# Gelu, expert weights and diagonals in two halves of eight rows, with VectorE's small steps moved behind later dot products

## The chip, the cores and the metric

The kernel runs on one core of one Trainium2 chip. Its engines are TensorE (matrix products, into PSUM), VectorE, ScalarE (functions of one argument), GpSimd (here above all the issuer of indirect DMAs) and SyncE (issuer of plain DMAs). Each runs its own instructions in order; they wait for each other through semaphores. The metric is the device time of one execution in microseconds (us), lower is better.

## The reference

Two decoder layers over 512 tokens of width 1024, all in float32. The change lies in the second half of each layer, PEER, a layer of 16,384 experts of one neuron each, of which every token picks 16 for each of 8 heads:

```python
def block(args):
    xb, ib, gb = args
    a = jax.nn.gelu(jnp.einsum('td,tkd->tk', xb, expert_u[ib]), approximate=False)
    return jnp.einsum('tk,tkd->td', a * gb, expert_v[ib])
...
for i in range(DEPTH):
    mix = hybrid_mixer(x, w_in[i], conv_w[i], b_if[i], ret_norm_g[i], mlstm_norm_g[i], w_out[i])
    x1 = layer_norm(DN_ALPHA * x + mix, ln1_g[i], ln1_b[i])
    y = peer(x1, peer_wq[i], peer_keys[i], peer_u[i], peer_v[i])
    e = jax.nn.sigmoid(x1 @ ple_wg[i] + ple_bg[i]) * (p[i] @ ple_wp[i])
    x = layer_norm(DN_ALPHA * x1 + y + e, ln2_g[i], ln2_b[i])
```

`ib` holds the expert numbers a token picked, `gb` the softmax weights of its picks. Each pick costs one row of `expert_u` and one of `expert_v`, 4 KB each: 512 x 128 x 2 rows a layer, 537 MB.

## The kernel before

**Tiles and loops.** Tokens lie on the 128 partitions, so there are 4 blocks of 128. A *pair* n = 0 to 31 is one block (n // 8) and one head (n % 8); it has 16 *rows* k, the 16 picks of every token. For one row GpSimd gathers a 128 x 1024 tile of U (`gather_u`, L558) and later one of V (`gather_v`, L567), 512 KB each, into two rings of 8 tiles (`UR`, `VR`). A U slot is free again when VectorE has done its dot product (semaphore `u_free`), a V slot when TensorE (`v_free`) or VectorE (`v_added`) has used it.

**One pair through the engines.** VectorE multiplies each U tile with the block's x and sums along the row (`dot_products`, L1066; x stands in PSUM as `xps`, put there by ScalarE's `copy_x`, L613 and L614, once a block). After 16 dots ScalarE takes Gelu of all 16 (L607), VectorE multiplies with the softmax weights (`weights`, L1088 and L1091), and ScalarE makes from each of the 16 columns a diagonal 128 x 128 matrix (L795). TensorE multiplies the diagonal with the V tile and adds up in PSUM (L1610, two products of 512 columns a row, four records in the trace), over all 8 heads of a block. GpSimd's order is fixed: in loop n it issues u(n+1,k), v(n,k) for k = 0 to 15. So V rows of pair n arrive while VectorE does the dots of pair n+1.

**What lies between.** In loops 2 to 9 TensorE first computes the query and score products for one head of the other three blocks (L1416, L1437), which ScalarE copies out (L627, L642) after the diagonals. VectorE's top-16 search for pairs n+2 to n+4 is cut in small steps, some behind each dot (`halves_step`, `pairs_step`). In pairs 2 to 7 every fourth V row (3, 7, 11, 15; `on_vector`) is not taken by TensorE: VectorE adds it, times its weight, to `yv` (`add_row`, L1108), behind the dot of the same k of the next pair. In pair 31 it takes every second row. `PLE_AT` names eight pairs in which the embedding term e is computed for half a block's columns: TensorE (L1571 to L1575) before the pair's V rows, ScalarE's sigmoid (L805), VectorE's multiply and add (`add_ple`, L1339, L1343 or L1345) after the pair's dots. `LN_AT` names three pairs with a final LayerNorm; ScalarE's square root for it stands at the end of the loop. `add_y` (L1325, L1327) takes the finished sum of a block out of PSUM. In pair 1 ScalarE's loop begins with the queries and scores of heads 4 to 7 and the transposes of three blocks, before Gelu.

The two ends that the prediction follows are these: `gelu` waits for `u_free` at 16 (n + 1), and `weights(n)` stands at the end of `dot_products(n)` and waits for `gelu_done`:

```python
e.wait_ge(gelu_done, n + 1)
e.scalar_tensor_tensor(wgt[:, n % 2, :], act_d, grec[:, 0:1], gexp[:, b, :], ALU.mult, ALU.mult).then_inc(wgt_ready, 1)
```

## Time and profile before

| What | us |
|---|---|
| timed runs: median of 3 (lowest, highest) | 3441.97 (3438.99, 3443.26) |
| profiled execution: span, first to last instruction | 3781.1 |
| TensorE matmul busy | 3004.2 |
| VectorE busy | 2120.8 |
| GpSimd busy | 1984.4 |
| ScalarE busy | 676.8 |

The page gives no time around the span. Its mean granted TensorE clock is 0.933 of full. The DMA engines moved 1174.41 MB, 311 GB/s over the span; the 2,048 gathers carry 1073.87 MB of it. In the page's slices one sees two stretches with little DMA traffic (the mixers, about 300 us each at the start of a layer) and two long ones near full (PEER, about 1,500 us each). The chain that ended last is spread over all engines (TensorE 27%, VectorE 18%, GpSimd 16%, issue 15%, DMA 9%), as it is where a ring of buffers couples them.

### The profile page before, as it was taken

How to read it: one execution, taken by the hardware profiler on the slowest of the kernel's cores; microseconds unless marked ns; L12 is line 12 of the kernel's file. 1: busy time of each engine (PE TensorE's matmuls, PEld its weight loads, DVE VectorE, ACT ScalarE, POOL GpSimd, SP SyncE). 2: the span in 40 equal slices, each digit the busy share in tenths (PEclk: the TensorE clock that was granted, in tenths of full speed). 3: DMA queues.
4: the chain of work that ended last, by engine and by line, in shares of the span. 5: the costliest groups of instructions: out<-in, count | busy, mean ns of one | idle time of the engine just before them, and what ended most of it. 6: DMA issues, size and time to landing. Idle time of an engine off the chain costs nothing.

```text
span 3781.1 us, 25835 instructions
## 1 busy us (share of the span) xinstructions
PE 3004.2 (79%) x7696; PEld 1341.3 (35%) x7696; DVE 2120.8 (56%) x4948; ACT 676.8 (18%) x1658; POOL 1984.4 (52%) x2100
## 2 busy tenths in 40 slices
PE   8999777778778888777699987777777788887776
PEld 4555433333223323222245544333322233333222
DVE  1447665575555655665424476665656555656654
ACT  1331111111111112111013211111111111121110
POOL 0014455566665666666500145555566666666665
PEclk9999888889999999999999998888899999999999
DMA  4127899998999999999831278998899999989998
GB/s 153 67 70 256 313 342 344 346 350 338 399 368 351 355 384 355 348 371 367 336 129 67 70 269 316 353 347 339 335 363 407 363 352 363 385 329 362 371 370 321
DMA packets 360799, 1174.41 MB, mean 311 GB/s; under 512 B 36946, under 2 KB 75986, under 8 KB 360404
## 3 DMA queue, kind: packets, MB, share of 16 engines
q0 software_dynamic: 294912, 1073.87, 74.7%
q1 hardware_dynamic: 63284, 98.59, 7.6%
q8 instruction: 61, 1.00, 0.1%
q10 hardware_dynamic: 2464, 0.31, 0.1%
q14 instruction: 78, 0.64, 0.0%
HBM read 1170.54 MB, written 2.10 MB: 310 GB/s over the span
## 4 chain that ended last, share of the span: by engine, by line
PE 27%; DVE 18%; POOL 16%; issue 15%; another core or an unknown queue 11%; DMA 9%; ACT 4%; DVEq 1%; ACTq 0%; SPq 0%; POOLq 0%
DVE arena L1066 10%; POOL arena L567 9%; PE bank L1610 8%; POOL arena L558 8%; DMA arena<-in_peer_v,rows 5%; PE bank L1389 5%; DMA arena<-in_peer_u,rows 4%; PE yv L1389 3%; ACT arena L795 3%; PE bank L1416 2%; PE yv L1547 1%; PE bank L1437 1%; PE yv L1467 1%; PE bank L1547 1%
## 5 line engine op out<-in xcount | busy, mean ns | idle before, releaser
L1610 PE MATMUL bank<-arena 128*128 128x512 f32 x3840 | 1906.7, 637 | 523.0 <-DMA arena<-in_peer_v,rows 318.4
L1066 DVE CUSTOM_DVE_ANT_0 arena<-arena,xps 128x1024 f32<-128x1024 f32 x1024 | 1237.4, 1214 | 629.3 <-DMA arena<-in_peer_u,rows 464.2
L567 POOL DMA_INDIRECT arena<-in_peer_v,rows x1024 | 974.6, 952 | 714.1 <-issue 281.8
L1610 PEld LDWEIGHTS bank<-arena 128*128 128x128 f32 x3840 | 719.3, 200 | 1696.4 <-issue 938.4
L558 POOL DMA_INDIRECT arena<-in_peer_u,rows x1024 | 972.5, 950 | 552.1 <-issue 293.0
L607 ACT ACTIVATE arena<-arena 128x16 f32<-128x16 f32 x64 | 13.9, 218 | 1897.9 <-issue 1160.9
L795 ACT ACTIVATE arena<-keep,arena 128x128 f32<-128x128 f32 x960 | 294.2, 388 | 299.1 <-remote 147.8
L1416 PE MATMUL bank<-xT,arena 128*128 128x128 f32 (+1 forms) x1024 | 250.2, 399 | 57.4 <-issue 55.5
L1416 PEld LDWEIGHTS bank<-xT,arena 128*128 128x128 f32 x1024 | 165.3, 203 | 132.5 <-issue 72.3
L1389 PE MATMUL bank<-arena,xT 128*128 128x512 f32 (+1 forms) x448 | 187.1, 573 | 6.4 <-DMA arena<-in_w_in 4.3
L1389 PE MATMUL yv<-arena,xT 128*128 128x512 f32 (+1 forms) x320 | 132.6, 569 | 0.0
L1437 PE MATMUL bank<-arena 128*128 128x128 f32 x192 | 46.9, 434 | 100.5 <-ACTq L628 90.8
L1339 DVE TENSOR_TENSOR arena<-arena,bank 128x512 f32<-128x512 f32 x16 | 11.0, 687 | 195.3 <-ACTq L806 118.1
L1389 PEld LDWEIGHTS bank<-arena,xT 128*128 128x128 f32 x448 | 84.9, 193 | 99.8 <-issue 90.7
L1571 PE MATMUL bank<-arena,xT 128*128 128x512 f32 x256 | 112.5, 592 | 0.0
L544 POOL TENSOR_TENSOR arena<-arena,normg 128x256 f32<-128x256 f32 x8 | 5.8, 726 | 189.7 <-ACTq L719 189.7
L1437 PEld LDWEIGHTS bank<-arena 128*128 128x128 f32 x192 | 42.2, 329 | 119.2 <-ACTq L628 106.0
L1066 DVE DVE_READ_ACCUMULATOR2_ANT arena<- 128x1 f32 x1024 | 84.1, 82 | 0.0
L1389 PEld LDWEIGHTS yv<-arena,xT 128*128 128x128 f32 x320 | 60.9, 195 | 62.1 <-issue 60.5
L540 POOL MEMSET arena<- 128x3 f32 x8 | 0.4, 101 | 142.5 <-PE xps L1485 142.5
L1571 PEld LDWEIGHTS bank<-arena,xT 128*128 128x128 f32 x256 | 48.6, 190 | 61.2 <-issue 61.2
L1547 PE MATMUL yv<-arena,xT 128*128 128x512 f32 x160 | 69.7, 592 | 0.0
(288 smaller groups left out, 1966.1 us busy)
## 6 DMA issues: line engine op xcount, KB each, us to landing
arena<-in_peer_wq SPq DMA_DIRECT2D x32, 1024.0 KB
arena<-in_w_in SPq DMA_DIRECT2D x12, 2048.0 KB, 8.0
arena<-in_peer_u,rows POOLq DMA_INDIRECT x1024
arena<-in_peer_v,rows POOLq DMA_INDIRECT x1024
arena<-in_w_out SPq DMA_DIRECT2D x4, 2048.0 KB, 8.2
arena<-in_ple_wg SPq DMA_DIRECT2D x4, 2048.0 KB
arena<-in_mixer SPq DMA_DIRECT2D x2, 2112.0 KB, 19.4
ln<-in_ln SPq DMA_DIRECT2D x8, 512.0 KB, 7.9
```

Source lines behind the costliest of these rows:

```text
L558: e.indirect_dma_start(urow[i % UR], None, a["peer_u"], bass.IndirectOffsetOnAxis(ap=rows[:, n % RR, k:k + 1], axis=0)).then_inc(u_in[i % ...
L567: e.indirect_dma_start(vrow[i % VR], None, a["peer_v"], bass.IndirectOffsetOnAxis(ap=rows[:, n % RR, k:k + 1], axis=0)).then_inc(v_in[i % ...
L607: e.activation(act_d, dots[:, n % 2, :], ACT.Gelu).then_inc(gelu_done, 1)
L795: e.activation(diag[:, k, :], ident, ACT.Copy, scale=wgt[:, n % 2, k:k + 1]).then_inc(diag_ready, 1)
L1066: e.tensor_tensor_reduce(r, r, xps[:, :], 1.0, 0.0, ALU.mult, ALU.add, dots[:, n % 2, k:k + 1]).then_inc(u_free, 1)
L1389: ins = e.matmul(ps[:, 0:w], xT[:, k, i * P:(i + 1) * P], wt[:, k, :], start=(k == 0), stop=(k == KT - 1))
L1416: ins = e.matmul(ps[:, at:at + hi - lo], wq[m % 2][:, k, n * P:(n + 1) * P], xT[:, k, lo:hi], start=(k == 0), stop=(k == KT - 1))
L1437: ins = e.matmul(ps[:, b * NKEYS:(b + 1) * NKEYS], qT[:, s, b * P:(b + 1) * P], keys[m % KR][:, s, :], start=True, stop=True)
L1467: ins = e.matmul(ps[:, :], wt[:, k, i * P:(i + 1) * P], xT[:, k, :], start=(k == 0), stop=(k == KT - 1))
L1547: ins = e.matmul(ps[:, :], xT[:, k, b * P:(b + 1) * P], wt[:, k % 4, side * 512:(side + 1) * 512], start=(k == 0), stop=(k == KT - 1))
L1571: e.matmul(ps[:, :], xT[:, k, b * P:(b + 1) * P], wg[:, k, :], start=(k == 0), stop=False)
L1610: ins = e.matmul(bank[m][:, :], diag[:, k, :], vrow[i % VR][:, m * 512:(m + 1) * 512], start=(h == 0 and k == 0), stop=(h == PH - 1 and k ...
```

## The change

- Gelu, `weights` and the diagonals are done for rows 0 to 7 and 8 to 15 apart (`HALF`), the first half already within the pair. In `dot_products(n)` VectorE does `weights(n, 0)` behind dot 9 and `weights(n-1, 1)` behind dot 1 (`WEIGHT_ROW`); only pairs 0 and 31 differ.
- The embedding's `add_ple` stands behind dot 5 of the next pair (`PLE_ROW`).
- In pairs 2 to 7 VectorE takes V rows 0, 4, 8, 12, and adds row k behind dot k + 3 (`VLAG`).
- ScalarE's order in loop n: Gelu and diagonals of the first half, Gelu of the second, `copy_x` of the next block (before: at the head of the next loop), the LayerNorm's square root (before: at the loop's end), diagonals of the second half.

```diff
@@ -67,2 +67,4 @@
 SR, RR, PC = 5, 6, D // 2
+HALF = TOPK // 2
+WEIGHT_ROW, VLAG, PLE_ROW = 1, 3, 5
 
@@ -462,6 +464,6 @@
         def on_vector(i):
-            return i % VD == VD - 1 if VFIRST <= i < VLAST else i >= VHALF and i % 2 == 1
+            return i % VD == 0 if VFIRST <= i < VLAST else i >= VHALF and i % 2 == 1
 
         def vector_rows(i):
-            return max(0, min(i, VLAST) - VFIRST) // VD + max(0, i - VHALF) // 2
+            return (max(0, min(i, VLAST) - VFIRST) + VD - 1) // VD + max(0, i - VHALF) // 2
 
@@ -603,6 +605,19 @@
 
-                def gelu(n):
+                def gelu(n, s):
 
-                    e.wait_ge(u_free, (n + 1) * TOPK)
-                    e.activation(act_d, dots[:, n % 2, :], ACT.Gelu).then_inc(gelu_done, 1)
+                    lo, hi = s * HALF, (s + 1) * HALF
+                    e.wait_ge(u_free, n * TOPK + hi)
+                    e.activation(act_d[:, lo:hi], dots[:, n % 2, lo:hi], ACT.Gelu).then_inc(gelu_done, 1)
+
+                def diagonals(n, s):
+
+                    e.wait_ge(wgt_ready, 2 * n + s + 1)
+                    for k in range(s * HALF, (s + 1) * HALF):
+                        if on_vector(n * TOPK + k):
+                            continue
+                        if n > 0 and on_vector((n - 1) * TOPK + k):
+                            e.wait_ge(v_free, tensor_rows((n - 1) * TOPK + k))
+                        elif n > 0:
+                            e.wait_ge(v_free, tensor_rows((n - 1) * TOPK + k) + 1)
+                        e.activation(diag[:, k, :], ident, ACT.Copy, scale=wgt[:, n % 2, k:k + 1]).then_inc(diag_ready, 1)
 
@@ -754,3 +769,4 @@
                             choice(1)
-                            gelu(0)
+                            gelu(0, 0)
+                            gelu(0, 1)
                         elif i == (3, 0):
@@ -763,4 +779,2 @@
                 for n in range(PAIRS):
-                    if n % PH == 0 and n > 0:
-                        copy_x(n // PH)
                     steps = pair_steps(n)
@@ -785,12 +799,12 @@
                     if n > 0:
-                        gelu(n)
-                    e.wait_ge(wgt_ready, n + 1)
-                    for k in range(TOPK):
-                        if on_vector(n * TOPK + k):
-                            continue
-                        if n > 0 and on_vector((n - 1) * TOPK + k):
-                            e.wait_ge(v_free, tensor_rows((n - 1) * TOPK + k))
-                        elif n > 0:
-                            e.wait_ge(v_free, tensor_rows((n - 1) * TOPK + k) + 1)
-                        e.activation(diag[:, k, :], ident, ACT.Copy, scale=wgt[:, n % 2, k:k + 1]).then_inc(diag_ready, 1)
+                        gelu(n, 0)
+                    diagonals(n, 0)
+                    if n > 0:
+                        gelu(n, 1)
+                    if n % PH == PH - 1 and n + 1 < PAIRS:
+                        copy_x(n // PH + 1)
+                    if n in LN_AT:
+                        e.wait_ge(var_ready, 3 + NB + LN_AT[n])
+                        e.sqrt(rstd[:, 0:1], rstd[:, 0:1]).then_inc(std_ready, 1)
+                    diagonals(n, 1)
                     for step, i in steps:
@@ -810,5 +824,2 @@
                         choice(n + 3)
-                    if n in LN_AT:
-                        e.wait_ge(var_ready, 3 + NB + LN_AT[n])
-                        e.sqrt(rstd[:, 0:1], rstd[:, 0:1]).then_inc(std_ready, 1)
                 e.wait_ge(var_ready, 2 + 2 * NB)
@@ -1079,14 +1090,21 @@
                             pairs_step([n + 2, n + 3], k, i + 1)
-                        if n > 0 and on_vector((n - 1) * TOPK + k):
-                            add_row(n - 1, k, i + 1)
-                    e.drain()
-
-                def weights(n):
-
-                    b = n % NB
-                    e.wait_ge(gexp_ready, n + 1)
-                    e.reciprocal(grec, gsum[:, b:b + 1])
-                    e.drain()
-                    e.wait_ge(gelu_done, n + 1)
-                    e.scalar_tensor_tensor(wgt[:, n % 2, :], act_d, grec[:, 0:1], gexp[:, b, :], ALU.mult, ALU.mult).then_inc(wgt_ready, 1)
+                        if n > 1 and k == WEIGHT_ROW:
+                            weights(n - 1, 1)
+                        if n > 0 and k == HALF + WEIGHT_ROW:
+                            weights(n, 0)
+                        if n > 0 and k >= VLAG and on_vector((n - 1) * TOPK + k - VLAG):
+                            add_row(n - 1, k - VLAG, i + 1)
+                        if k == PLE_ROW and n - 1 in PLE_AT:
+                            add_ple(PLE_AT[n - 1])
+                    e.drain()
+
+                def weights(n, s):
+
+                    b, lo, hi = n % NB, s * HALF, (s + 1) * HALF
+                    if s == 0:
+                        e.wait_ge(gexp_ready, n + 1)
+                        e.reciprocal(grec, gsum[:, b:b + 1])
+                        e.drain()
+                    e.wait_ge(gelu_done, 2 * n + s + 1)
+                    e.scalar_tensor_tensor(wgt[:, n % 2, lo:hi], act_d[:, lo:hi], grec[:, 0:1], gexp[:, b, lo:hi], ALU.mult, ALU.mult).then_inc(wgt_ready, 1)
                     e.drain()
@@ -1102,3 +1120,3 @@
                         e.drain()
-                    elif i == VFIRST + VD - 1:
+                    elif i == VFIRST:
                         e.tensor_scalar(yv[:, :], vrow[i % VR], w, None, ALU.mult).then_inc(v_added, 1)
@@ -1351,3 +1369,4 @@
                         first_norm(1)
-                        weights(n)
+                        weights(n, 0)
+                        weights(n, 1)
                         halves_first([2, 3])
@@ -1356,8 +1375,6 @@
                         pairs_second([2, 3])
-                    else:
-                        weights(n)
+                    elif n == PAIRS - 1:
+                        weights(n, 1)
                     if n % PH == 0 and n > 0:
                         add_y(n // PH - 1)
-                    if n in PLE_AT:
-                        add_ple(PLE_AT[n])
                     if n in LN_AT:
@@ -1603,2 +1620,4 @@
                         i = n * TOPK + k
+                        if k % HALF == 0:
+                            e.wait_ge(diag_ready, tensor_rows(i + HALF))
                         if on_vector(i):
@@ -1606,6 +1625,4 @@
                         e.wait_ge(v_in[i % VR], (l * (PAIRS * TOPK // VR) + i // VR + 1) * 16)
-                        if k % (2 * VD) == 0:
-                            e.wait_ge(diag_ready, tensor_rows(i + 2 * VD))
                         for m in range(2):
-                            ins = e.matmul(bank[m][:, :], diag[:, k, :], vrow[i % VR][:, m * 512:(m + 1) * 512], start=(h == 0 and k == 0), stop=(h == PH - 1 and k == (TOPK - 2 if b in (0, NB - 1) else TOPK - 1)))
+                            ins = e.matmul(bank[m][:, :], diag[:, k, :], vrow[i % VR][:, m * 512:(m + 1) * 512], start=(h == 0 and k == 0), stop=(h == PH - 1 and k == (TOPK - 2 if b == NB - 1 else TOPK - 1)))
                         ins.then_inc(v_free, 1)
```

Three places show what the edits do to the order. The first is VectorE in pair 1, from its tenth dot (the row with u_in1) in the change, and from its fourteenth (u_in5) before; a dot is the row `arena<-arena,xps` and the `128x1` behind it; `RECIPROCAL` and the product behind it are the weights. Before:

```order
L1066 ISA arena<-arena,xps 128x1024 [waits u_in5]
L1066 ISA arena 128x1
L991 TENSOR_TENSOR arena<-arena 128x512 [waits u_free]
L1066 ISA arena<-arena,xps 128x1024 [waits u_in6]
L1066 ISA arena 128x1
L996 CAST arena<-topi 128x64 [waits u_free]
L1066 ISA arena<-arena,xps 128x1024 [waits u_in7]
L1066 ISA arena 128x1
L1088 RECIPROCAL arena<-arena 128x1 [waits gexp_ready]
L1091 SCALAR_TENSOR_TENSOR arena<-arena 128x16 [waits gelu_done]
L1066 ISA arena<-arena,xps 128x1024 [waits u_in0]
```

In the change (other line numbers, same functions):

```order
L1077 ISA arena<-arena,xps 128x1024 [waits u_in1]
L1077 ISA arena 128x1
L969 MAX_INDEX topi<-arena 128x8 [waits u_free]
L970 MAX_INDEX topi<-arena 128x8
L973 MAX_INDEX topi<-arena 128x8 [waits u_free]
L974 MAX_INDEX topi<-arena 128x8
L1106 RECIPROCAL arena<-arena 128x1 [waits gexp_ready]
L1109 SCALAR_TENSOR_TENSOR arena<-arena 128x8 [waits gelu_done]
L1077 ISA arena<-arena,xps 128x1024 [waits u_in2]
L1077 ISA arena 128x1
L977 MATCH_REPLACE arena<-arena 128x128 [waits u_free]
```

The wait for `gelu_done` stood behind the sixteenth dot (u_in7) and stands behind the tenth; six dots of pair 1 now come after it.

The second is VectorE at the end of pair 17, with the embedding's multiply and add (the product that waits for `ple_gate`). Before, it comes behind the last dot (u_in7) and the weights:

```order
L1066 ISA arena<-arena,xps 128x1024 [waits u_in7]
L1066 ISA arena 128x1
L1088 RECIPROCAL arena<-arena 128x1 [waits gexp_ready]
L1091 SCALAR_TENSOR_TENSOR arena<-arena 128x16 [waits gelu_done]
L1339 TENSOR_TENSOR arena<-arena,bank 128x512 [waits work_full1,ple_gate]
L1343 TENSOR_TENSOR acc<-acc,arena 128x512
L1066 ISA arena<-arena,xps 128x1024 [waits u_in0]
```

In the change it is in pair 18, behind that pair's sixth dot (u_in5):

```order
L1030 MAX arena<-arena 128x8 [waits u_free]
L1031 MAX arena<-arena 128x8
L1077 ISA arena<-arena,xps 128x1024 [waits u_in5]
L1077 ISA arena 128x1
L1034 MAX_INDEX pos<-arena 128x8 [waits u_free]
L1357 TENSOR_TENSOR arena<-arena,bank 128x512 [waits work_full1,ple_gate]
L1361 TENSOR_TENSOR acc<-acc,arena 128x512
L1077 ISA arena<-arena,xps 128x1024 [waits u_in6]
```

Six dots and their small steps moved ahead of it. The third is ScalarE in loop 7 and at the head of loop 8: Gelu, diagonals, the copies of query and score, and the two copies of x. Before:

```order
L607 ACTIVATE arena<-arena 128x16 [waits u_free]
L795 ACTIVATE arena<-keep,arena 128x128 [waits v_free,wgt_ready]
L795 ACTIVATE arena<-keep,arena 128x128 [waits v_free] x11
L627 COPY arena<-bank 128x384 [waits work_full0,work_full1]
L627 COPY arena<-bank 128x384 [waits work_full1]
L642 COPY arena<-bank 128x3x128 [waits work_full0]
L642 COPY arena<-bank 128x3x128 [waits work_full1]
L613 COPY xps<-x 128x512 [waits u_free]
L614 COPY xps<-x 128x512
L607 ACTIVATE arena<-arena 128x16 [waits u_free]
L795 ACTIVATE arena<-keep,arena 128x128 [waits v_free,wgt_ready]
```

In the change:

```order
L610 ACTIVATE arena<-arena 128x8 [waits u_free]
L622 ACTIVATE arena<-keep,arena 128x128 [waits v_free,wgt_ready]
L622 ACTIVATE arena<-keep,arena 128x128 [waits v_free] x5
L610 ACTIVATE arena<-arena 128x8 [waits u_free]
L628 COPY xps<-x 128x512 [waits u_free]
L629 COPY xps<-x 128x512
L622 ACTIVATE arena<-keep,arena 128x128 [waits v_free,wgt_ready]
L622 ACTIVATE arena<-keep,arena 128x128 [waits v_free] x5
L642 COPY arena<-bank 128x384 [waits work_full0,work_full1]
L642 COPY arena<-bank 128x384 [waits work_full1]
L657 COPY arena<-bank 128x3x128 [waits work_full0]
L657 COPY arena<-bank 128x3x128 [waits work_full1]
```

The copies of x (`xps<-x`) moved from behind the diagonals and four copies of query and score to just behind the second Gelu.

## Rows read from the trace of the kernel before

**Rows 1.** The page: busy us (share, instructions) and GB/s in 40 slices.
```profile
PE 3004.2 (79%) x7696; PEld 1341.3 (35%) x7696; DVE 2120.8 (56%) x4948; ACT 676.8 (18%) x1658; POOL 1984.4 (52%) x2100
GB/s 153 67 70 256 313 342 344 346 350 338 399 368 351 355 384 355 348 371 367 336 129 67 70 269 316 353 347 339 335 363 407 363 352 363 385 329 362 371 370 321
```
**Rows 2.** Windows (busy us by engine, clock, DMA share, GB/s): a calm stretch, and one around a pause.
```profile
1044.00:1076.00 32.00, 23.83 (x49) 8.13 (x48) 22.01 (x47) 4.82 (x16) 24.07 (x27) 1.00 1.01 396
1079.00:1095.00 16.00, 10.55 (x23) 3.67 (x22) 9.21 (x30) 3.66 (x7) 8.75 (x10) 1.00 0.84 293
```
**Rows 3.** Timeline (start us, us, engine, line; idle before, releaser), GpSimd, u(17,15).
```profile
1196.64 0.94 POOL L558 DMA_INDIRECT arena<-in_peer_u,rows  x1 [0.31 <-issue]
```
**Rows 4.** Timeline, VectorE and GpSimd, behind a pause.
```profile
1081.47 0.09 DVE L966 MATCH_VALUE_LOAD arena<-arena 128x8 f32 x1 [2.97 <-issue]
1081.71 0.94 POOL L567 DMA_INDIRECT arena<-in_peer_v,rows  x1 [3.77 <-issue]
```
**Rows 5.** Timeline, VectorE, end of pair 17: last dot, embedding's multiply.
```profile
1203.11 1.22 DVE L1066 CUSTOM_DVE_ANT_0 arena<-arena,xps 128x1024 f32<-128x1024 f32 x1 [1.33 <-DMA arena<-in_peer_u,rows]
1225.03 0.69 DVE L1339 TENSOR_TENSOR arena<-arena,bank 128x512 f32<-128x512 f32 x1 [20.12 <-ACTq L806]
```
**Rows 6.** Timeline, GpSimd, u(18,8).
```profile
1228.13 0.94 POOL L558 DMA_INDIRECT arena<-in_peer_u,rows  x1 [4.31 <-DVE arena L1066]
```
**Rows 7.** Waits (us, times, longest), GpSimd, pairs 16 to 25, layers one and two.
```profile
POOL arena L558 <- DVE arena L1066: 30.6, 14, 6.3
POOL arena L558 <- DVE arena L1066: 34.0, 21, 7.3
```
**Rows 8.** Timeline, TensorE, pair 17: embedding and its bias product.
```profile
1206.23 7.03 PE L1571 MATMUL bank<-arena,xT 128*128 128x512 f32 x16
1213.19 1.12 PE L1572 MATMUL bank<-arena,keep 1*128 1x512 f32 x2
```
**Rows 9.** Timeline, ScalarE, pair 17: Gelu and sigmoid.
```profile
1204.37 0.22 ACT L607 ACTIVATE arena<-arena 128x16 f32<-128x16 f32 x1 [27.18 <-issue]
1224.37 0.60 ACT L805 ACTIVATE arena<-bank 128x512 f32<-128x512 f32 x1
```
**Rows 10.** Timeline, VectorE, pair 1: dots 10 and 15, weights.
```profile
406.50 1.20 DVE L1066 CUSTOM_DVE_ANT_0 arena<-arena,xps 128x1024 f32<-128x1024 f32 x1
418.96 1.21 DVE L1066 CUSTOM_DVE_ANT_0 arena<-arena,xps 128x1024 f32<-128x1024 f32 x1
436.68 0.24 DVE L1091 SCALAR_TENSOR_TENSOR arena<-arena 128x16 f32<-128x16 f32 x1 [12.71 <-ACT arena L607]
```
**Rows 11.** Timeline, ScalarE, pair 1: a query's copy, and Gelu.
```profile
413.95 0.37 ACT L623 COPY arena<-bank 128x256 f32<-128x256 f32 x1 [12.23 <-remote]
436.42 0.22 ACT L607 ACTIVATE arena<-arena 128x16 f32<-128x16 f32 x1
```
**Rows 12.** Timeline, GpSimd, u(2,2) and u(2,9).
```profile
409.22 0.93 POOL L558 DMA_INDIRECT arena<-in_peer_u,rows  x1 [0.30 <-issue]
444.80 0.94 POOL L558 DMA_INDIRECT arena<-in_peer_u,rows  x1 [0.30 <-issue]
```
**Rows 13.** Waits of the whole span.
```profile
PE bank L1610 <- ACT arena L795: 59.2, 21, 7.9
DVE arena L1091 <- ACT arena L607: 26.1, 2, 13.4
```
**Rows 14.** Timeline, VectorE and GpSimd, first dot of pair 8 and u(8,8).
```profile
751.41 1.22 DVE L1066 CUSTOM_DVE_ANT_0 arena<-arena,xps 128x1024 f32<-128x1024 f32 x1 [23.32 <-ACT xps L614]
752.91 0.93 POOL L558 DMA_INDIRECT arena<-in_peer_u,rows  x1 [12.05 <-DVE arena L1066]
```
**Rows 15.** Timeline, TensorE and GpSimd: first V row of pair 6, v(6,8); first V row of pair 7.
```profile
699.29 4.05 PE L1610 MATMUL bank<-arena 128*128 128x512 f32 x8
701.90 0.94 POOL L567 DMA_INDIRECT arena<-in_peer_v,rows  x1 [8.68 <-PE bank L1610]
...
749.44 6.72 PE L1610 MATMUL bank<-arena 128*128 128x512 f32 x13
```

## The prediction

> **What bounds the kernel now.** I read the busy rows of the page first: the expert stage of each layer (from about 320 to 1876 us, and again from 2200) keeps the 16 DMA engines near full, up to 407 GB/s [rows 1]. A window of a calm stretch shows what full means: 396 GB/s at a DMA share of 1.01 [rows 2]. Then GpSimd's timeline: it issues 2,048 gathers of 512 KB, and in calm stretches one every 1.24 us, 0.94 busy and 0.30 between [rows 3]. A pair of gathers (one U row, one V row) therefore cannot start faster than every 2.49 us, and at 396 GB/s its 1.05 MB take 2.65. The two limits stand so close that a GpSimd stall is not made up: what GpSimd waits beyond 0.30 us is lost, except where another chain is later anyway. The question for each edit is which GpSimd wait it ends or starts.
>
> One thing must be set aside. At 1081.5 us GpSimd, VectorE and ScalarE all come back from a pause, GpSimd having idled 3.77 us, VectorE 2.97 [rows 4], while VectorE waited only for its own dot product; in the 16 us around it DMA moves 293 GB/s [rows 2]. The profiled span is 3781.1 us (the page gives nothing around it), the median of the timed runs 3441.97: 339 us less. Such pauses recur through the whole stage, and 339 us is 90 of them at 3.77; so I take most of them to belong to the profiled execution. Gaps in the trace then bound a gain from above, and I rebuild the two chains that matter without pauses.
>
> **The change, part by part.** Notation: dot(n,k) is row k of pair n, u(n,k) and v(n,k) its gathers. GpSimd issues u(n+1,k), then v(n,k); each has a ring of eight.
>
> *Embedding later (8 pairs a layer).* At the end of pair 17 the last dot starts at 1203.11 and ends 1.2 later; the embedding's multiply starts at 1225.03 after 20.12 us of idle time [rows 5], and the next dot 1.6 us behind it. GpSimd had room to u(18,7) and then waited 4.31 us for that dot [rows 6]. By the view of waits over the ten pairs 16 to 25 these waits are 30.6 us (14) in layer one and 34.0 (21) in layer two [rows 7]; less 35 x 0.30, 54 us in all. That is the upper bound of this part: after the change VectorE has the multiply behind dot(n+1,5), 15 us later, and nothing stalls. Without pauses: TensorE starts the embedding at 1206.23, its bias product ends at 1213.19 + 1.12 = 1214.3 [rows 8], the sigmoid takes 0.60 (it stands at 1224.37 here, 10 us after its input) [rows 9], the two VectorE steps 1.6: the next dot would start at 1216.5 and end at 1217.7. GpSimd's u(18,8) would be due nine steps after u(17,15), at 1196.6 [rows 3]: 1196.6 + 9 x 2.49 = 1219.0. So in an execution free of pauses this stall is nothing, with 1.3 us to spare. Bounds 0 and -54. The timed runs have most of the 339 us less, not surely all, and eight to ten near misses a layer turn into stalls with any delay; I take -22, between the ends and nearer zero.
>
> *VectorE's wait for Gelu moved up: the price.* Weights of the first half now stand behind dot(n,9), so dots 10 to 15 of the same pair queue behind a Gelu. In steady pairs ScalarE has been idle before it, 27.18 us in pair 17 [rows 9], and answers at once. Pair 1 is different: there ScalarE reaches its Gelu only behind four queries, four score copies and three transposes, at 436.42 [rows 11]. VectorE now runs dots 10 to 15 at 406.50 to 418.96 and waits 12.71 us after all of them [rows 10]. After the change it waits behind dot(1,9), from about 406.4, and dot(1,10) starts where dot(2,0) stands now, about 437. The u ring is what this stops: u(2,2) was issued at 409.22 and needs dot(1,10), so it comes at about 438.3. Now GpSimd stops only at u(2,8) and v(1,8), and u(2,9) comes at 444.80 [rows 12]; after, it comes at 438.3 + 7 x 2.49 = 455.7: 11 us late. TensorE's V rows of pair 1 then wait for their rows. Both layers have this wait (26.1 us in two) [rows 13]: +22. Without pauses ScalarE's Gelu would come sooner: its copy at 413.95 alone idled 12.23 us [rows 11]. If it comes at 424, the stall of u(2,2) is 425.8 - 409.2 = 16.6 us and the old one about nothing until u(2,8), due 6 x 2.49 = 15 us after u(2,2); if at 418, 10.6 us and none: 11 to 15, nearly the same. Lower bound +5 a layer (the queries' weight loads fill part of the hole), upper +15: +10 to +30 for both, taken +21.
>
> *copy_x before the diagonals.* At the end of pair 7 the next dot waits 23.32 us and GpSimd 12.05 [rows 14]. But v(7,8) behind it waits for TensorE as in every pair from 2 to 9: v(6,8) came at 701.90, 2.6 us after TensorE's first V row at 699.29, and in pair 7 that row stands at 749.44 [rows 15]. So v(7,8) would come at 752.0; now it comes one issue after 752.91, at 754.15. I take 3.5 a layer, bounds 0 and 10: -7. At 15 to 16 and 23 to 24 GpSimd never stalled: 0.
>
> *VectorE's V rows.* In pairs 2 to 7 VectorE takes rows 0, 4, 8, 12 instead of 3, 7, 11, 15, after the same dots 3, 7, 11, 15, so 24 adds a layer stay where they are. v(n,8) no longer waits for TensorE but v(n,9) does, and TensorE's last row is 15 instead of 14, with the next query right behind it: one pair-step of 2.49 won, the same lost. 0; bounds -2.5 and +2.5 for each of 12 pairs, -30 to +30, near zero because both ends belong to one loop. The lag also holds a V slot until dot k+3; the ring leaves five rows, GpSimd runs three ahead (8 us over 2.49): no wait.
>
> *Instructions.* 62 more Gelus of 0.22 us and as many small products of 0.24 [rows 9, 10]: ScalarE is 18% busy [rows 1]; the gaps between dots hide them. The number of table loads does not change; if one came with each half, 62 x 1.28 would sit on ScalarE beside 27 us of idle time, still 0. TensorE's waits for a diagonal (59.2 us in 21) [rows 13] go where the pair starts, but the V ring covers nearly all of them: -4, bounds 0 and -10.
>
> Sum on the profile: -22 + 21 - 7 + 0 - 4 = -12 us. Carried over one to one: 3442 - 12 = **3430 us**.
>
> The Trainium skill ("DMA: Bandwidth & Descriptors", section Bandwidth) puts the HBM side of a core's HBM to SBUF stream at about 358 GB/s. The trace does not agree: 396 and 407 GB/s stand in its rows. By that rule the stage would have no room at all, and the answer would be the third rival below.
>
> **Rivals.** (1) *The wait in pair 1 decides; the change is slower.* VectorE sits behind dot(1,9) in both layers and the embedding stalls were the profiler's own. For it: the rebuilt chain with its 1.3 us to spare, and a wait that no ring covers. +21 - 7 = +14: 3456 us. It decides as soon as the embedding part brings under 14 us. (2) *The stalls of the trace are real in the timed runs.* Then -54 - 7 - 4 + 21 = -44: 3398. For it: 65 us of GpSimd waits by name; against it: 339 us that the timed runs do not have. (3) *DMA is the floor.* With backlog enough the queues hide both stalls and gains: within 7 us of 3442. Windows at 396 GB/s speak for it, the page's 350 in most slices against it.
>
> **Chances.** Forecast 0.35 (3420 to 3440), rival 1 0.27, rival 2 0.20, rival 3 0.18. A difference under 0.2%, 7 us, is what measuring this kernel cannot tell from none. Faster: 0.20 + most of 0.35 = 0.50; within: 0.26; slower: 0.24. All low bounds together give about 3370, all high ones 3472 with the V rows at zero; the range with 8 in 10 is 3388 to 3462.
>
> **What would show it.** Right: in the profile after, VectorE's second-half weights and the embedding multiply have no idle time to speak of before them, and GpSimd's waits for VectorE in pairs 16 to 25 are under 15 us a layer; in pair 1 the first half's weights show 25 to 30 us of idle time, and GpSimd waits at u(2,2), about 25 us in the profile. TensorE's first V row of pairs 3 to 8 is still about 24 us behind its last one. Wrong: if GpSimd does not stop in pair 1, or if the embedding's stalls turn up at v(n,8) as waits for TensorE, which has some 9 us of embedding before each such pair's rows. A time over 3449 means rival 1; under 3405, rival 2.

## The result, and the profile after

| | us |
|---|---|
| before, 20 runs | 3439.67 (3434.43 to 3443.30) |
| after, 20 runs | 3445.84 (3440.58 to 3448.96) |
| ratio | 1.0018, 95% interval 1.0011 to 1.0024 |

The change makes the kernel 6 us slower. That is under the 0.2% named ahead, but the interval excludes no change. 3430 was forecast. The time lies in the range, on the other side of before.

The profiled execution of the changed kernel spans 3445.8 us and has no pauses. A second one of the kernel before, taken for the comparison, has none either: 3437.2 us, not 3781.1. Below, "before" is this undisturbed profile. Its page, busy times and slices, and then those of after [rows 1]:

```profile
PE 2918.5 (85%) x7696; PEld 1282.2 (37%) x7696; DVE 2136.1 (62%) x4948; ACT 669.9 (19%) x1658; POOL 1983.2 (58%) x2100
GB/s 142 75 49 182 358 406 405 404 407 394 407 409 397 407 407 400 409 409 409 358 129 73 39 218 361 405 405 405 407 399 407 409 394 408 403 404 405 409 409 343
```
```profile
PE 2920.6 (85%) x7696; PEld 1287.8 (37%) x7696; DVE 2160.6 (63%) x5012; ACT 688.7 (20%) x1722; POOL 1983.9 (58%) x2100
GB/s 142 75 49 186 345 407 404 405 398 408 407 409 406 406 407 400 407 409 409 336 135 73 32 212 353 406 405 405 396 409 407 410 402 408 404 403 405 409 409 333
```

From the sixth slice on, to the last but one of the stage, both stand at 394 to 410 GB/s: the 350 of rows 1 was the paused execution's average. What differs is the ramp (358 to 345 in the fifth slice, 361 to 353 in the second layer's) and the slice in which the stage ends (358 to 336, 343 to 333). Windows of the ramp, before and after (length, busy time of five engines, clock, DMA share, GB/s), and of the ten pairs of the embedding:

```profile
375.00:450.00 75.00, 60.03 (x252) 34.40 (x250) 55.90 (x130) 13.11 (x34) 46.44 (x49) 0.95 0.94 355
1105.00:1444.00 339.00, 305.62 (x666) 120.93 (x666) 225.14 (x528) 72.42 (x180) 242.48 (x258) 0.99 1.02 406
```
```profile
375.00:450.00 75.00, 60.11 (x248) 33.92 (x248) 53.10 (x128) 15.48 (x42) 38.29 (x41) 0.95 0.92 341
1107.00:1446.00 339.00, 305.74 (x667) 121.53 (x667) 233.92 (x536) 74.78 (x189) 245.03 (x257) 0.99 1.02 405
```

The loss is in pair 1 [rows 10 to 12]. Timelines of ScalarE, VectorE and GpSimd in the changed kernel:

```profile
413.68 0.21 ACT L610 ACTIVATE arena<-arena 128x8 f32<-128x8 f32 x1
```
```profile
413.92 0.23 DVE L1109 SCALAR_TENSOR_TENSOR arena<-arena 128x8 f32<-128x8 f32 x1 [10.99 <-ACT arena L610]
```
```profile
415.78 0.93 POOL L560 DMA_INDIRECT arena<-in_peer_u,rows  x1 [10.58 <-DVE arena L1077]
```

ScalarE comes to the half Gelu at 413.68, VectorE has stood 10.99 us for it, and GpSimd 10.58 at u(2,2). In the kernel before VectorE has done all sixteen dots by then. ScalarE waits 0.85 us for the last of them, and VectorE's weights come without idle time before them:

```profile
414.00 0.22 ACT L607 ACTIVATE arena<-arena 128x16 f32<-128x16 f32 x1 [0.85 <-DVE arena L1066]
```
```profile
414.30 0.24 DVE L1091 SCALAR_TENSOR_TENSOR arena<-arena 128x16 f32<-128x16 f32 x1
```

The embedding's part did what it says, and the waits changed their name [rows 7]. GpSimd's waits (us in total, times, longest) in pairs 16 to 25 of layer one, before and then after:

```profile
POOL arena L558 <- DVE arena L1066: 34.7, 28, 9.6
POOL arena L567 <- PE bank L1610: 7.9, 26, 0.3
```
```profile
POOL arena L569 <- PE bank L1627: 34.4, 36, 8.1
POOL arena L560 <- DVE arena L1077: 6.0, 15, 1.7
```

42.6 us before, 40.4 after. (The 7.9 us in 26 are nothing but the 0.30 us that stand before every issue.) At pair 16 a stop of 8.36 us at u(17,8) turned into one of 7.93 at v(16,8), the issue behind it, within a microsecond:

```profile
1079.23 0.94 POOL L558 DMA_INDIRECT arena<-in_peer_u,rows  x1 [8.36 <-DVE arena L1066]
```
```profile
1079.74 0.94 POOL L569 DMA_INDIRECT arena<-in_peer_v,rows  x1 [7.93 <-PE bank L1627]
```

When the last V gather of a pair lands shows what all this is worth (read from the records of the two traces, us):

```
layer one   pair 2   pair 31  between    layer two  pair 2   pair 31  between
before       499.4    1712.2   1212.8               2209.8   3422.5   1212.7
after        502.3    1715.1   1212.8               2218.4   3431.2   1212.8
```

From pair 2 to pair 31 both take the same time to 0.1 us. What is lost is lost before pair 2: 2.9 us in layer one and, counted from the landing of its first pair, 2.1 in layer two. The remaining 3.6 us of these two profiles' 8.6 lie between the layers, where the change edits nothing; they go with the granted clock, as shown behind the terms of the prediction.

### The profile page after: what moved, and what is told of

Read it like the earlier page. It is cut to its first block, busy times and chain, and to the rows that moved or that the text cites. A ratio compares the mean times of both kernels' runs of the same rounds, so it can differ in the third digit from the quotient of the medians.

```text
span 3445.8 us, 26089 instructions
## 1 busy us (share of the span) xinstructions
PE 2920.6 (85%) x7696; PEld 1287.8 (37%) x7696; DVE 2160.6 (63%) x5012; ACT 688.7 (20%) x1722; POOL 1983.9 (58%) x2100
## 4 chain that ended last, share of the span: by engine, by line
PE 39%; DMA 32%; POOL 17%; issue 7%; DVE 4%; ACT 1%; DVEq 0%; ACTq 0%; SPq 0%; POOLq 0%
DMA arena<-in_peer_v,rows 22%; PE bank L1627 12%; POOL arena L569 9%; DMA arena<-in_peer_u,rows 8%; POOL arena L560 8%; PE bank L1433 5%; PE bank L1406 5%; PE yv L1406 4%; PE bank L1588 3%; PE yv L1564 2%; DVE arena L1077 2%; PE yv L1484 1%; PE bank L1564 1%; PE bank L1592 1%; DMA arena<-in_w_in 1%
## 5 line engine op out<-in xcount | busy, mean ns | idle before, releaser
L1627 PE MATMUL bank<-arena 128*128 128x512 f32 x3840 | 1867.2, 624 | 454.1 <-DMA arena<-in_peer_v,rows 436.9
L1627 PEld LDWEIGHTS bank<-arena 128*128 128x128 f32 x3840 | 696.2, 194 | 1608.5 <-DMA arena<-in_peer_v,rows 811.4
L610 ACT ACTIVATE arena<-arena 128x8 f32<-128x8 f32 x128 | 27.0, 211 | 1301.5 <-DVE arena L1077 1301.5
L1433 PE MATMUL bank<-xT,arena 128*128 128x128 f32 (+1 forms) x1024 | 227.8, 381 | 1.9 <-ACTq L762 1.5
L1433 PEld LDWEIGHTS bank<-xT,arena 128*128 128x128 f32 x1024 | 156.0, 191 | 75.7 <-issue 9.6
L537 POOL TENSOR_TENSOR arena<-arena 128x512 f32<-128x512 f32 x8 | 10.1, 1263 | 95.4 <-DVEq L1163 95.4
L1126 DVE SCALAR_TENSOR_TENSOR yv<-arena,yv 128x1024 f32<-128x1024 f32 x46 | 58.9, 1280 | 1.3
```

Of the source, the lines that this page charges most:

```text
L610: e.activation(act_d[:, lo:hi], dots[:, n % 2, lo:hi], ACT.Gelu).then_inc(gelu_done, 1)
L1126: e.scalar_tensor_tensor(yv[:, :], vrow[i % VR], w, yv[:, :], ALU.mult, ALU.add).then_inc(v_added, 1)
L1433: ins = e.matmul(ps[:, at:at + hi - lo], wq[m % 2][:, k, n * P:(n + 1) * P], xT[:, k, lo:hi], start=(k == 0), stop=(k == KT - 1))
L1627: ins = e.matmul(bank[m][:, :], diag[:, k, :], vrow[i % VR][:, m * 512:(m + 1) * 512], start=(h == 0 and k == 0), stop=(h == PH - 1 and k ...
```

## Experiments

Each ratio is to runs of the kernel before on the same chip.

**1. The kernel before again.** 

> The kernel before, once more, for a profile to set beside that of the changed kernel, and as the measure of what 'no change' looks like. Both theories: 3440 us, ratio to before 1.000 within 0.1%. The trace of before that the prediction rested on had a span of 3781 us with 339 us of pauses in it; the theory is that these were that one execution's own, so a second profile of the same program spans 3438 us or so, its DMA slices are flat at 400 to 410 GB/s like those of the changed kernel, and GpSimd's waits for VectorE behind the embedding (30.6 and 34.0 us a layer in rows 7) shrink to under 10 us a layer. Rival: they were real, the waits stay at 30 us a layer, and then moving the embedding must have gained some 20 us that something else ate.

3440.23 us, ratio 1.0004 (0.9995 to 1.0014); span 3437.2, and the slices above. The pauses were that one execution's own. But the waits stayed (34.7 and, in layer two, 34.6 us), so neither side had it: they are real, and yet, as experiment 4 shows, their end brings no time.

**2. The wait of pair 1 taken away.**

```diff
-                        if n > 0 and k == HALF + WEIGHT_ROW:
+                        if n > 1 and k == HALF + WEIGHT_ROW:
...
+                    elif n == 1:
+                        weights(n, 0)
```

> The changed kernel with one thing undone: in the second pair the weights of the first eight rows come behind all sixteen dot products again, instead of behind the tenth. Theory A (that wait is the cause of the loss): GpSimd's stop at the u gather of the third pair's row 2 (10.6 us at 416 us and 10.0 us at 2132 us) goes, and 16 to 21 us come off: 3425 to 3430 us, which is below before too. Theory B (the DMA queues take it back: they are the floor from pair 3 on and the stop lies beside work that has to wait anyway): the stop goes but less than 5 us of the time, 3441 to 3446 us. Theory C (V rows are the cause): no change, 3446 us.

3440.07 us, ratio 1.0004 (0.9995 to 1.0013): before's time again. The stop at u(2,2) is gone. It took 5.8 us with it: theory A had the cause right and the size three times too large, and theory B, under 5 us because the DMA queues take the rest back, was the nearer one. All other parts of the change together are worth nothing that can be measured.

**3. The V rows as before** (rows 3, 7, 11, 15; `VLAG` 0; the stop flag at row 14 in the first block). 

> The changed kernel with VectorE's V rows as before: rows 3, 7, 11, 15 of pairs 2 to 7, each added right behind the dot product of its own number, instead of rows 0, 4, 8, 12 three dots later. Theory A (the wait in the second pair is the whole loss, the V rows cost nothing): GpSimd's 30 us of waits for the adds of V rows go, and the time stays within 3 us of 3446. Theory C (the slots that are held three dots longer delay the gathers behind them): 10 to 20 us come off, 3426 to 3436 us. Rival of both: row 0 on VectorE lets TensorE start later and end at row 15, so undoing it takes a gain away, 3450 us or more.

3447.01 us, ratio 1.0023 (1.0012 to 1.0034): beside after's 3445.84 nothing that eight runs between 3441.60 and 3452.68 could tell. Theory A had this right. GpSimd's waits from 460 to 770 us, after and then here:

```profile
POOL arena L569 <- PE bank L1627: 19.0, 17, 4.5
POOL arena L569 <- DVE yv L1126: 16.6, 11, 3.2
```
```profile
POOL arena L569 <- PE bank L1627: 35.8, 21, 5.9
```

35.6 us and 35.8: again the same sum under another name.

**4. The embedding's move alone,** on the kernel before:

```diff
+                        if k == 5 and n - 1 in PLE_AT:
+                            add_ple(PLE_AT[n - 1])
...
-                    if n in PLE_AT:
-                        add_ple(PLE_AT[n])
```

> The kernel before with one part of the change alone: the embedding's adds behind the sixth dot product of the next pair. In the undisturbed profile of before, GpSimd waits 60.2 us for VectorE in pairs 16 to 25 of both layers, 2.9 us in the changed kernel. Theory A (from the third pair on the DMA queues are the bound at 405 to 409 GB/s, so GpSimd's stops there cost nothing): those waits go to under 10 us, its waits for TensorE grow by about as much, and the time stays at 3438 to 3442 us. The prediction's own view (22 us for this move): 3418 us.

The reverse, only this part undone in the changed kernel, has no time: there the sigmoid that the adds need stands behind diagonals whose weights VectorE makes only after the adds, in the next pair, so the two wait for each other for ever.

3441.26 us, ratio 1.0002 (0.9993 to 1.0011). The term of 22 us is zero within 4 us. GpSimd's waits in pairs 16 to 25 of layer one, 34.5 us in all, now mostly for TensorE:

```profile
POOL arena L567 <- PE bank L1610: 27.9, 32, 8.1
POOL arena L558 <- DVE arena L1066: 6.6, 8, 4.5
```

**5. The wait of pair 1 three dots later** (`k == HALF + 4` where n is 1). 

> The changed kernel with the wait of the second pair three dot products later: its first-half weights stand behind the thirteenth dot product instead of the tenth, all else as changed. Each of these dots has two steps of the choice beside it, some 2.3 us, so VectorE reaches the wait about 9 us later and stands 2 us instead of 11.0. Theory A (a stop of GpSimd costs only what the DMA queues' backlog doesn't cover, and in the changed kernel 10.6 us of stop cost 3 us a layer): the stop at the third pair's row 2 shrinks under 3 us and the time goes to before's, 3438 to 3442 us. Theory D (not the stop but the halving itself, the extra waits and instructions, costs the 6 us): 3444 to 3447 us.

3442.15 us, ratio 1.0006 (0.9997 to 1.0015). VectorE waits 4.6 us, not 2, and GpSimd stops 3.4 us, at u(2,5) (2.5 in layer two):

```profile
413.50 0.23 DVE L1109 SCALAR_TENSOR_TENSOR arena<-arena 128x8 f32<-128x8 f32 x1 [4.61 <-ACT arena L610]
```
```profile
415.36 1.27 POOL L560 DMA_INDIRECT arena<-in_peer_u,rows  x1 [3.38 <-DVE arena L1077]
```

Most of the 6 us is gone though the halves are all there: theory D falls.

**6 and 7. ScalarE's square root ahead of head 4's copies,** on the changed kernel and on the one before. It isn't part of the change; it closes a hole that both have.

```diff
                         for b in range(2, NB):
-                            if b == NB - 1:
-                                copy_q((4, 0))
-                                copy_s((4, 0))
                             e.wait_ge(var_ready, 3 + b)
                             e.sqrt(rstd[:, 0:1], rstd[:, 0:1]).then_inc(std_ready, 1)
+                        copy_q((4, 0))
+                        copy_s((4, 0))
```

> The changed kernel with one edit of its own that is not part of the change: in the second pair ScalarE takes the square root of the last block's norm ahead of its two copies of the query and scores of head 4, not behind them. In the profiles VectorE stands 8.7 us for that root in both kernels, GpSimd 13.5 us at the second pair's u row 13, and the DMA engines are idle from 387 to 394 us. Theory A (DMA is the bound, so time comes only from where DMA stands idle): the gap closes, but here Gelu of the second pair still comes when it did (behind ScalarE's other copies, at 413.7 us), so the stop at the third pair's row 2 grows from 10.6 toward 19 us and gives most of it back: 3436 to 3444 us. Rival (the two stops don't touch each other): 8 us a layer, 3430 us.

3460.82 us, ratio 1.0062 (1.0049 to 1.0076): slower than either side had it. GpSimd's stop at u(1,13) shrinks from 13.81 us to 4.75, but VectorE then stands 7.19 us for scores and comes to its wait for Gelu only 2.4 us earlier (400.5 instead of 402.9). Gelu comes 5.9 us later, at 419.60. The third query's product sets that: its weights, asked for within 1 us of the same time, land 11.0 us after their issue instead of 6.4, and it ends at 407.65 instead of 401.73. Timelines of VectorE, GpSimd and TensorE:

```profile
419.85 0.23 DVE L1108 SCALAR_TENSOR_TENSOR arena<-arena 128x8 f32<-128x8 f32 x1 [19.36 <-ACT arena L610]
```
```profile
421.71 0.94 POOL L560 DMA_INDIRECT arena<-in_peer_u,rows  x1 [20.00 <-DVE arena L1076]
```
```profile
401.65 6.00 PE L1432 MATMUL bank<-xT,arena 128*128 128x128 f32 x32 [4.93 <-DMA arena<-in_peer_wq]
```

> The kernel before with the same edit: the square root ahead of the copies of head 4 in the second pair. Theory A (DMA the bound from the second pair to the last; a gap in it closed early is kept to the end): 7 to 8 us a layer, 3424 to 3427 us, with the landings of the V rows of every later pair 7 to 8 us earlier in the first layer. Rival (the time is set by TensorE's and VectorE's own work in pairs 2 to 9, with DMA only busy because it is asked early): less than 3 us in all, 3437 to 3440 us.

3435.69 us, ratio 0.9989 (0.9980 to 0.9998): a gain, and about a quarter of what theory A had. The hole at 387 us narrows (267 to 328 GB/s in the window from 375 to 400), but the next 50 us fall from 400 to 375. Here too VectorE now waits for Gelu in pair 1, behind its sixteenth dot, and GpSimd stops 7.29 us at u(2,8), which needs the dot behind that wait:

```profile
420.96 0.24 DVE L1090 SCALAR_TENSOR_TENSOR arena<-arena 128x16 f32<-128x16 f32 x1 [10.31 <-ACT arena L607]
```

**8 and 9. DMA taken off the bound.** In both kernels the V gathers of pairs 8 to 30 fetch 2 KB a row, and TensorE multiplies that half twice: the kernels leave out the other half of these rows, and their output is not the reference's.

```diff
+                    w = 512 if 8 <= n < PAIRS - 1 else 1024
-                    e.indirect_dma_start(vrow[i % VR], None, a["peer_v"], ...
+                    e.indirect_dma_start(vrow[i % VR][:, 0:w], None, (a["peer_v"] if w == 1024 else a["peer_v"].rearrange("r (h c) -> (r h) c", h=2)), ...
```

> The kernel before with the V gathers of pairs 8 to 30 halved (each fetches 2 KB a row instead of 4, from the first half of the table, and TensorE multiplies the same half twice, so the values of these pairs are not the reference's). It takes the DMA bound away: a pair's 16.8 MB at 408 GB/s, 41 us, become 12.6 MB, 31 us. What is left is GpSimd's own issue, 32 gathers by 0.94 + 0.30 us = 39.7 us a pair. Theory A: with DMA out of the way a stop of GpSimd costs its full length, so the kernel before keeps its 30 us a layer of waits for VectorE in pairs 16 to 25: about 2 x (23 x 1.8 - 25) = 33 us come off, 3395 to 3415 us.

> The changed kernel with the same halved V gathers in pairs 8 to 30. Theory A: here the waits for VectorE are 3 us a layer and those for TensorE no longer follow from DMA's pace, so the changed kernel is now 15 to 50 us faster than the kernel before with halved gathers: the embedding's move was worth about what the prediction gave it (22 us) or more, but only where DMA isn't the bound. Rival (the waits moved from VectorE to TensorE for a reason of their own, TensorE being late by the embedding's matmuls): both halved kernels within 8 us of each other.

3359.34 us (ratio 0.9763, 0.9748 to 0.9778) and 3364.52 (0.9773, 0.9757 to 0.9789), four runs each. The rival had the difference right (5 us, within its 8), and theory A was wrong in an instructive way: I had expected the 30 us of waits to stay in the halved kernel before and to cost their length. They are not there. Waits of GpSimd in pairs 16 to 25, halved kernel before:

```profile
POOL arena L568 <- PE bank L1611: 8.2, 27, 0.3
POOL arena L558 <- DVE arena L1067: 4.6, 15, 0.3
```

None is longer than the 0.3 us that every issue has. A pair takes 40.5 us (1084.4 to 1449.0 for nine), a little over the 32 issues of 1.24. GpSimd waits for VectorE or TensorE there only because DMA is slower than its issue: the rings must fill, and it stops at whichever row frees its slot last. The median time from issue to landing shows the queue, before and then the halved one:

```profile
arena<-in_peer_u,rows POOLq DMA_INDIRECT x1024, 10.5
arena<-in_peer_v,rows POOLq DMA_INDIRECT x1024, 10.7
```
```profile
arena<-in_peer_u,rows POOLq DMA_INDIRECT x1024, 5.6
arena<-in_peer_v,rows POOLq DMA_INDIRECT x1024, 5.0
```

**10 to 12. A version that beats both.** First the two repairs of 2 and 6 together:

> The changed kernel with the two repairs together: the second pair's first-half weights behind all its dot products, and ScalarE's square root ahead of the copies of head 4. Theory A: no wait for Gelu is left in the second pair in either form (the kernel before with the early root still had stops of 5.3 and 7.3 us at the third pair's u rows 1 and 8, partly for it), so it is below before and at or below the 3435.7 us of the kernel before with the early root: 3430 to 3436 us. If the stop at row 8 is VectorE's own work (two steps of the choice behind each dot product), it is the same as that kernel within 2 us.

3435.50 us, ratio 0.9992 (0.9983 to 1.0001): the same as experiment 7. In it VectorE still stands 8.41 us for Gelu. Then, on the changed kernel with the early root, ScalarE's order in pair 1 mended, so that Gelu comes ahead of the later copies, with VectorE's weights two dots later (ScalarE's old calls for pair 1 go; not shown):

```diff
                             copy_s(i)
+                            if n == 1 and i == (5, 0):
+                                gelu(1, 0)
+                            elif n == 1 and i == (6, 0):
+                                diagonals(1, 0)
+                            elif n == 1 and i == (7, 0):
+                                gelu(1, 1)
...
-                        if n > 1 and k == WEIGHT_ROW:
+                        if n > 1 and k == (3 if n == 2 else WEIGHT_ROW):
...
-                        if n > 0 and k == HALF + WEIGHT_ROW:
+                        if n > 0 and k == (HALF + 3 if n == 1 else HALF + WEIGHT_ROW):
```

> The changed kernel with the early square root, and with ScalarE's own order in the second pair mended instead of VectorE's wait taken away: Gelu of the first half behind the copies of heads 4 and 5, its diagonals behind those of head 6, Gelu of the second half behind those of head 7, all ahead of the copies of x; VectorE's first-half weights behind the twelfth dot product and the second-half ones behind the fourth of the next pair. In the run with both repairs VectorE still stood 8.4 us at 413 us for Gelu (ScalarE came to it at 421.6 us), and the DMA engines ran at 320 to 370 GB/s from 393 to 448 us. Theory A (time comes only from where the DMA queues run short): that stop goes, the engines stay at 400 GB/s from 393 us on, and 1 to 3 us a layer come off beside 3435.5 us: 3429 to 3434 us. If it is 3435 us or more, what limits the ramp is VectorE's own work in the second pair and the order of waits in it no longer matters.

3434.25 us, ratio 0.9984 (0.9975 to 0.9993): just outside theory A's 3429 to 3434, and beside 3435.50 no difference clear of the scatter. Last, the norm of block 3 two dots later (`LN1_AT = {1: 2, 6: 3}`):

> The same kernel, with the norm of the last block two dot products later (behind the seventh of the second pair instead of the fifth). Theory A: GpSimd's stop of 4.7 us at the second pair's u row 13 shrinks, the DMA gap at 387 us (down to 4 GB/s in one us) closes, and up to 3 us a layer more come off: 3424 to 3432 us. Rival: the gap only moves behind the norm, and the time is that of the kernel above within 2 us.

3431.56 us, ratio 0.9978 (0.9969 to 0.9988): 8.6 us under before, 14 under after, as theory A had it at the slow end. It is 2.7 us under the kernel above, hardly more than the rival's 2. GpSimd's 4.7 us at u(1,13) did not go, though: 4.56 us stand two rows later, at u(1,15), so the gap in part moved. The ramp's window in this kernel:

```profile
375.00:450.00 75.00, 62.06 (x257) 36.30 (x255) 57.40 (x134) 14.96 (x41) 48.32 (x51) 0.98 1.00 379
```

379 GB/s where before has 355 and after 341. Landings of pairs 2 and 31 in layer one: 494.5 and 1707.8, 1213.3 us between, as in the other two: the gain, too, lies ahead of pair 2.

## Why the prediction was wrong

The mechanisms were mostly named; the sum went wrong by one choice. It took every GpSimd wait as lost time ("what GpSimd waits beyond 0.30 us is lost") and left the DMA floor to rival 3. By the runs the terms are 0 for all parts but the wait in pair 1, and 5.8 for that, where 6.2 us were measured.

- **The bound** failed. The two limits do stand close, 2.49 us against 2.65, but the slower one is DMA, and it alone counts: 1212.8 us from pair 2 to 31 in both kernels, whatever GpSimd waits, and some 80 us less in all when a quarter of the bytes of 23 pairs a layer is left out (experiments 8 and 9). The 350 of rows 1, which spoke against rival 3, came from pauses that the prediction had itself set aside.
- **Embedding, -22:** zero, alone (experiment 4) and within the change (experiment 2). The rebuilt chain, "nothing, with 1.3 us to spare", holds in the halved kernel, where no stop exceeds 0.3 us. It fails in the real one, as I read it, for a reason it left out: at DMA's pace (41.8 us a pair, 1212.8 by 29) the rows come later than GpSimd could issue them (39.7), and GpSimd must stop for the difference. And I then took -22 against my own chain. The sentence on what would make it wrong, the stalls turning up at v(n,8) as waits for TensorE, is what the profile shows.
- **VectorE's wait in pair 1, +21:** the mechanism and the place u(2,2) are right, and the stop without pauses (10.6 to 16.6 us) at its low end: 10.6 and, in layer two, 10.0. Its cost is 5.8 us in all (3445.84 less 3440.07), not 21, and under the lowest bound of 10. The step that failed is that everything behind the stop comes later by its length. Three sizes of the stop:

```
mean stop a layer   cost a layer                       not charged
 2.9 (experiment 5) (3442.15 - 3440.07) / 2 =  1.0      1.9
10.3 (after)        (3445.84 - 3440.07) / 2 =  2.9      7.4
19.8 (experiment 6) (3460.82 - 3435.50) / 2 = 12.7      7.1
```

  The first row is within the measurement's error. In the second the stop takes the place of a later one. Here is GpSimd at v(2,8) in layer one, before and then after:

```profile
471.56 0.93 POOL L567 DMA_INDIRECT arena<-in_peer_v,rows  x1 [9.83 <-PE bank L1610]
```
```profile
471.69 0.94 POOL L569 DMA_INDIRECT arena<-in_peer_v,rows  x1 [0.30 <-issue]
```

  So the gather of v(2,15) is issued at the same time in both (488.94 and 489.08 us), but it lands 10.4 us later before and 12.9 after. GpSimd's time was made up; the DMA engines' was not. They ran short behind u(2,2): u(2,1) had landed 8.2 us after its issue, u(2,2) took 4.4. The third row's 7.1 is not the same thing measured twice. The kernel it is compared with, experiment 10, has stops of 5.36 and 4.02 us of its own at u(2,8) and v(1,8), which are gone here. How much of a stop a backlog of gathers covers isn't shown.
- **copy_x, -7, and TensorE's waits for diagonals, -4:** the waits went as described. VectorE's 36.6 us for `xps` in the profile of before [rows 14] have no row in the one of after, and TensorE's 47.7 us for diagonals [rows 13] became 16.1, with 17.9 on its weight loads. Neither brought time. (For copy_x the prediction's own rows give 2.15 us a layer, 754.15 less 752.0; the 3.5 was a choice.) These waits of the whole span, before and then after:

```profile
DVE arena L1066 <- ACT xps L614: 36.6, 4, 13.1
PE bank L1610 <- ACT arena L795: 47.7, 30, 6.0
```
```profile
PEld bank L1627 <- ACT arena L622: 17.9, 8, 5.3
PE bank L1627 <- ACT arena L622: 16.1, 4, 5.0
```

- **V rows, 0:** right as a sum, wrong in its reason. "No wait" was false: GpSimd waits for VectorE's late adds, 16.6 us in layer one, and TensorE's first V row in pairs 2 to 9 stands 12.4 us behind its last, not 24, in both kernels. Both are hidden by the same floor.
- **Extra instructions, 0:** right; experiment 2 has all of them and runs as before. They are 64 on each engine, not 62 (ScalarE 1658 to 1722, VectorE 4948 to 5012).
- **Rivals.** By experiment, rival 3 was right (within 7 us of before), with rival 1's mechanism as its small remainder. It had 0.18. The Trainium skill's rule behind it ("DMA: Bandwidth & Descriptors", section Bandwidth, about 358 GB/s) gave the right kind of limit at a height that isn't this case's. The same section gives that figure as a core's share when both cores of the memory domain stream, and up to 425 GB/s for a core alone. The trace has 404 GB/s from 500 to 1712 us.

The 3.6 us between the layers go with TensorE's granted clock. Windows from layer one's last landing to layer two's first gather, before and after:

```profile
1712.00:2028.00 316.00, 296.38 (x1097) 162.84 (x1097) 120.37 (x353) 77.52 (x135) 19.17 (x25) 0.97 0.25 87
```
```profile
1715.00:2034.00 319.00, 299.62 (x1097) 165.42 (x1096) 119.79 (x353) 77.36 (x135) 19.03 (x25) 0.95 0.25 86
```

In the thirteen profiles without pauses this stretch takes 314.0 to 318.7 us: 314.0 and 314.2 at a mean granted clock of 0.973, 315.3 to 316.3 at 0.968 (before among them), 317.5 to 318.7 at 0.952 (after, and also experiments 4 and 7, variants of before); the other three have 315.0 to 317.9 us at 0.957 to 0.962. The difference of the timed runs is not the clock's: the runs of experiment 3 have a median clock of 0.9755 and take 3447.01 us, those of experiment 2 have 0.975 and take 3440.07.

## What to carry to other kernels

When one resource sits at its limit from an early point to the end, waits elsewhere are its shadow: count what each engine waited before and after, and if only the name changed, nothing was gained. Look for time only where that resource runs short (here 75 us of ramp in each layer), and charge a stop with its length only after taking off the later stops whose place it takes. Judge a limit by an undisturbed stretch or a second profile, never by a mean over one that holds pauses.

## What was not expected of the hardware

- One program's two profiled executions span 3781.1 and 3437.2 us, while the 20 timed runs beside the changed kernel stay within 9 us.
- The 16 DMA engines hold 404 GB/s on the mean in 4 KB rows for 1.2 ms on end (500 to 1712 us of the undisturbed before), no slice under 394. With half of the rows at 2 KB and GpSimd as the bound they move 319 (1084 to 1449 us of experiment 8).
- With the gathers a few microseconds earlier a weight load lands later: the third query's product waits for its weights 4.93 us in experiment 6, 5.98 in 7 and 5.35 in 10, against 0.35 in the changed kernel. The clock granted in experiment 6 falls to 0.5 of full, the lower level, at 399.4 us, with TensorE idle since 396.7, and stays there to 406.2; the product then takes 6.00 us instead of 3.84 for the same 32 matmuls. The mean granted clock from 400 to 450 us is 0.87, against 0.93 in the changed kernel.
